# Shared expert and first routed expert in another order, with their tiles laid elsewhere, in a one-core decoder layer

## The chip, the cores and the metric

The kernel runs on one core of a Trainium2 chip. The metric is device time in microseconds (us). A core has TensorE (matrix products and transposes into eight PSUM banks), VectorE, ScalarE, GpSimd and SyncE, each with its own list of instructions in order; they wait for each other by semaphores. SyncE issues most of the transfers between HBM and SBUF; GpSimd issues those with indices (gather and scatter-add of rows).

## The reference

One decoder layer on 512 tokens of width 1024, float32: a token mixer (RG-LRU and S5), a layer norm, then a mixture of experts with a gated per-layer embedding (PLE) and a second layer norm. The change touches only the second half:

```python
y = jnp.einsum('tf,fd->td', jax.nn.silu(xt @ ws_gate) * (xt @ ws_up), ws_down)   # shared expert, F = 256
for c in range(N_EXPERTS // EXPERT_CHUNK):                                      # 64 experts, 8 per token
    ...
    hdn = jax.nn.silu(g) * u * combine[:, sl, None]
    y = y + jnp.einsum('tef,efd->td', hdn, w_down[sl])
ple = jax.nn.sigmoid(x @ ple_gate_w + ple_gate_b) * (p @ ple_w)
x = layer_norm(ALPHA * x + ffn + ple, ln2_g, ln2_b)
```

## The kernel before

SBUF is one arena of 53,200 float32 columns over 128 partitions; tiles are laid in it by hand at offsets, and many share columns at different times. The offsets that matter: `x_off` = 624, `late` = 4720, `b0` = 14960, `b1` = 26224, `m_off` = 37488, `sg_off` = 41584, `tail` = 46704. Each engine has one block of code, and its order is written out by hand.

Behind the first layer norm the tokens stand in four tiles of 128 (t = 0 to 3). TensorE then computes, per tile, the PLE gate (`ple_gate`, L923, 16 products in fp32, which the profile records as 32), the PLE value (`ple_value`, L935, 8 records), the router and the slot table (L951 to L970), and the shared expert's gate and up products (`sh_in`, L943, 16 records a tile, into banks 4, 5, 2, 3). VectorE's `ple(t)` writes `acc[:, t]`, the accumulator at `m_off`, from `ple_value(t)`; `ple_value(t)` waits for `ple(t - 1)`, as both use banks 2 and 3. The picks for the slot table are VectorE's `picks(t)`.

The shared expert goes on with silu on ScalarE (`sh_silu`, tile `sil`), its product with up on VectorE (`sh_hid`, tile `hdn`), a transpose on TensorE (`sh_turn`, through L698 like all transposes), a copy from the bank on VectorE (`sh_keep`, L1835, tile `hT`), the down product (`sh_out`, L1017, 8 records, banks 6 and 7) and two additions to `acc` on VectorE (`sh_add`). All of `sil`, `hdn` and `hT` have two buffers, at `b1` + 8192 to `b1` + 10240. SyncE then stores `acc` to `acc_dram` (L512), to which the routed experts' rows are added.

The routed experts run one after the other on up to 96 gathered rows. For expert e, with u = e mod 4: SyncE loads gate and up (2 MB, `gate_up`, L490) and down (1 MB, L493) into one of four buffers. ScalarE rounds gate and up to their high part (`gate_up_high`, four pieces of 128x1024, tile `gu_hi[u % 2]`), and VectorE subtracts to get the low part over the raw weights (`gate_up_low`). GpSimd gathers the rows, TensorE turns them (`x_turn`), and ScalarE and VectorE split them too (`rows_high`, `rows_low`). `gate_up` on TensorE is 24 products of 96 rows by 512 columns (L691 high by high, L693 high part by `rows_low`, L692 `gate_up_low` by high); then silu, the product with up and the gate, a turn (`hid_turn`), and `down` (L1057, 8 records). GpSimd adds the result rows to `acc_dram` by a scatter (`add_rows`, L642). TensorE's order in an expert is gate_up(e), x_turn(e + 1), down(e - 1), hid_turn(e). On ScalarE an expert is gate_up_high(e + 1), silu, rows_high(e + 1), y_kept(e - 1).

SyncE loads expert e + 4's gate and up when gate_up(e) is done and its down when down(e) is done, in one order. Expert 0 is loaded after the last `ple_value`, expert 1 after the last `ple`, experts 2 and 3 after the last `sh_in`.

The second high-part buffer, `gu_hi[1]`, lies at `m_off`, on the columns of `acc`. So ScalarE waits for `acc_stored` before expert(0, 0), whose first step is the high part of expert 1.

Lines of helpers: L1122 is ScalarE's `f`, L1344 and L1350 VectorE's `tt` and `stt`, L698 the transpose, L691 to L693 the three products of `mm3`.

Of the kernel before, what the change touches and what calls it, by code (L numbers as in the profile page):

```python
# [46 lines left out]
F = 256  # L47
# [25 lines left out]
def decoder_layer(nc, A, out):  # L73
# [9 lines left out]
    with ctx:  # L83
# [19 lines left out]
        def at(off, cols, rows_=P):  # L103
            assert off + cols <= COLS, (off, cols)
            return arena[0:rows_, off:off + cols]
# [8 lines left out]
        def part(name, off, n, width):  # L114

            assert off % 8 == 0 and off + n * width <= COLS
            t = nc.alloc_sbuf_tensor_at(name, (P, n * width), f32r, offset=arena_at + 4 * off)
            return t[:, :].rearrange("p (k t) -> p k t", k=n)
# [137 lines left out]
        xgT = at(tail + 4096, KD * SL).rearrange("p (k s) -> p k s", k=KD)  # L256
        xe_hi = part("rows_high", tail + 4096, KD, SL)
        xe_lo = part("rows_low", tail + 4096 + KD * SL, KD, SL)
        gu_hi = [part(f"gate_up_high{n}", o, 2 * KD, F) for n, o in enumerate((x_off, m_off))]
        gu_lo = [part(f"gate_up_low{n}", o, 2 * KD, F) for n, o in enumerate(gu_at)]  # L260
        heT = [at(b1 + 10240 + 512 * n, 2 * SL).rearrange("p (k s) -> p k s", k=2) for n in range(2)]
        hid_e = [at(tail + 5632 + n * F, F, SL) for n in range(2)]
        ohT = at(b1 + 10240, F).rearrange("p (k s) -> p k s", k=2)
        yb = [at(late + 8192 + n * D, D, SL) for n in range(2)]
        sil = [at(b1 + 8192 + n * F, F) for n in range(2)]
        hdn = [at(b1 + 8704 + n * F, F) for n in range(2)]
        hT = [at(b1 + 9216 + n * F, F).rearrange("p (k s) -> p k s", k=2) for n in range(2)]
        small = b0 + 8192

        def sc(off, cols, parts=P):  # L270
# [274 lines left out]
        def _(pool):  # L545
# [79 lines left out]
            def gather(e, u, n):  # L625

                nc.gpsimd.tensor_copy(idxcol[:, u:u + 1].bitcast(i32), idxT[:, bass.ds(e, 1)].bitcast(i32)).then_inc(S["slot_col"], 1)
                pool.wait_ge(S["slot_col"], n + 1)
                pool.sem_inc(S["col_seen"], 1)
                nc.gpsimd.indirect_dma_start(  # L630
                    out=xg[u], out_offset=None, in_=x1_dram,
                    in_offset=bass.IndirectOffsetOnAxis(ap=idxcol[:, u:u + 1].bitcast(u32), axis=0),
                    bounds_check=T - 1, oob_is_err=False).then_inc(s_gath[u], 16)
# [14 lines left out]
            pool.wait_ge(S["x1_stored"], 16 * TT)  # L648
            for u in range(4):
                gather(u, u, u)  # L650
            pool.wait_ge(S["acc_stored"], 16 * TT)

            def add_expert(i, u):
                pool.wait_ge(S["y_e_act"], 4 * i + u + 1)
# [3 lines left out]
            for u in range(4):  # L658
                pool.wait_ge(S["xT_e_put"], u + 1)
                gather(4 + u, u, 4 + u)  # L660
                if u:
                    add_expert(0, u - 1)
            with pool.Fori(1, E // 4 - 1) as i:
# [32 lines left out]
        def _(pe):  # L696
# [288 lines left out]
            ple_gate(0)  # L985
            ranks()
            ple_gate(1)
            ple_value(1)
            pe.wait_ge(S["shared_loaded"], 48)
            sh_in(0)  # L990
            ple_gate(2)
            slot_table()
            ple_value(2)
# [36 lines left out]
            def gate_up(i, u):  # L1030

                pe.wait_ge(S["gu_e_low"], 16 * i + 4 * u + 4)
                pe.wait_ge(S["xT_e_low"], 8 * i + 2 * u + 2)
                whi = gu_hi[u % 2].rearrange("p (w k) f -> p k w f", w=2)
                wlo = gu_lo[u % 4].rearrange("p (w k) f -> p k w f", w=2)
                for k in range(KD):
                    last = mm3(banks[2 + u % 2][0:SL, :], xe_hi[:, k], xe_lo[:, k], whi[:, k], wlo[:, k], k == 0, k == KD - 1)
                last.then_inc(S["g_e_put"], 1)
# [30 lines left out]
            sh_turn(1)  # L1069
            sh_out(0)  # L1070
            x_turn(0, 0)
            sh_out(1)
            sh_turn(2)
            sh_out(2)
            sh_turn(3)
            sh_out(3)
            expert(0, 0)
            pe.wait_ge(S["sh_done"], 2 * TT)
# [41 lines left out]
        def _(act):  # L1120
            def f(out_, in_, func, **kw):
                return nc.scalar.activation(out_, in_, func, **kw)  # L1122
# [152 lines left out]
            def gate_up_high(i, u):  # L1275
                act.wait_ge(s_wgu[u % 4], 32 * i + 32 * (u // 4 + 1))
                wait(act, S["g_e_put"], 4 * i + u - 1)
                for k in range(2):
                    for w in range(2):
                        ks = slice(KD * w + 4 * k, KD * w + 4 * k + 4)  # L1280
                        f(gu_hi[u % 2][:, ks], gu_raw[u % 4][:, ks], ACT.Copy).then_inc(S["gu_e_high"], 1)


            def y_kept(i, u):
# [15 lines left out]
            def sh_silu(t):  # L1300
                act.wait_ge(S["sh_put"], t + 1)
                need(act, "sh_hid", t - 1)
                f(sil[t % 2], banks[(4, 5, 2, 3)[t]][:, 0:F], ACT.Silu).then_inc(S["sh_silu"], 1)

            sh_silu(0)
            sh_silu(1)
            act.wait_ge(S["table_put"], 1)
            gate_up_high(0, 0)
            sh_silu(2)
            rows_high(0, 0)  # L1310
            sh_silu(3)
            act.wait_ge(S["acc_stored"], 16 * TT)
            for u in range(0, 5):
                expert(0, u)
            with act.Fori(1, E // 4 - 1) as i:
# [21 lines left out]
        def _(dve):  # L1337
# [5 lines left out]
            def tt(out_, a, b_, op):  # L1343
                return V_.tensor_tensor(out_, a, b_, op)  # L1344
# [506 lines left out]
            def gate_up_low(i, u):  # L1851
                for k in range(2):
                    for w in range(2):
                        ks = slice(KD * w + 4 * k, KD * w + 4 * k + 4)
                        dve.wait_ge(S["gu_e_high"], 16 * i + 4 * u + 2 * k + w + 1)
                        tt(gu_lo[u % 4][:, ks], gu_raw[u % 4][:, ks], gu_hi[u % 2][:, ks].bitcast(f32),
                           ALU.subtract).then_inc(S["gu_e_low"], 1)

            def y_kept(i, u):
# [86 lines left out]
```

## Time and profile before

| | |
|---|---|
| time, median of 3 runs | 1504.92 us (1503.16 to 1507.18) |
| profiled execution, its own time | 1510.24 us |
| its span | 1508.5 us |
| TensorE busy | 1421.3 us, 94% |
| VectorE busy | 877.7 us, 58% |
| ScalarE busy | 608.8 us, 40% |
| GpSimd busy | 431.1 us, 29% |
| mean granted TensorE clock | 0.972 |
| HBM read and written | 297.27 and 34.54 MB |

The profile is of one execution; its times are microseconds from the start of the span. "Idle before" is the time an engine stood still ahead of an instruction, and the arrow names what released it. The granted clock is a share of 2.4 GHz. A DMA share near 1 means that the 16 DMA engines are busy throughout. The span falls into the mixer (to about 613), the output projection and first norm, the PLE, router and shared expert (to about 820), the 64 experts (to about 1474) and the last norm.

### The profile page before, as it was taken

The numbers are of one execution on the slowest core, as the hardware profiler recorded it, in microseconds if no ns is written. First come the engines' busy times: TensorE is split into PE (matmuls) and PEld (weight loads), VectorE is DVE, ScalarE is ACT, GpSimd is POOL, SyncE is SP. The second block draws the span as 40 slices with busy tenths as digits, with TensorE's granted clock in tenths as the row PEclk, the third lists the DMA queues.
The fourth block names the chain that finished last, engine by engine and source line by source line (L and its number), as shares of the span: only waits on it lengthen the run. The fifth ranks groups of instructions, "written<-read, shape, count | busy, mean of one in ns | idle before, by whom it ended". The sixth has DMA issues, their size and how long they took to land.

```text
span 1508.5 us, 18646 instructions
## 1 busy us (share of the span) xinstructions
PE 1421.3 (94%) x6359; PEld 942.7 (62%) x6359; DVE 877.7 (58%) x1257; ACT 608.8 (40%) x850; POOL 431.1 (29%) x380
## 2 busy tenths in 40 slices
PE   6999899998999999999998999999999999999990
PEld 4466777675788888555544666666666666666650
DVE  3798868785600100247533667666766766666655
ACT  2215554536422222010011555555655555555440
POOL 0112525333454444000010232222233222333322
PEclk7999999999899999999999999999999999999996
DMA  8035242534233334730046799999999999999953
GB/s 246 2 112 81 74 71 72 86 63 102 63 98 98 91 98 157 306 141 12 0 169 260 256 353 354 359 367 359 363 362 363 370 367 371 359 363 367 353 160 125
DMA packets 140419, 315.77 MB, mean 209 GB/s; under 512 B 17888, under 2 KB 99472, under 8 KB 115088
## 3 DMA queue, kind: packets, MB, share of 16 engines
q1 hardware_dynamic: 126032, 281.50, 54.0%
q0 software_dynamic: 14336, 33.59, 9.5%
q8 instruction: 33, 0.54, 0.1%
q14 instruction: 18, 0.15, 0.0%
HBM read 297.27 MB, written 34.54 MB: 220 GB/s over the span
## 4 chain that ended last, share of the span: by engine, by line
PE 74%; issue 8%; DVE 7%; DMA 3%; POOL 2%; DVEq 2%; ACT 1%; POOLq 1%; SPq 0%; ACTq 0%
PE bank L691 14%; PE bank L693 14%; PE bank L692 14%; PE bank L1057 14%; PE bank L698 5%; PE bank L909 4%; DVE arena L1344 3%; DVEq L1341 2%; PE bank L923 2%; PE bank L943 2%; DMA gate_up<-moe_w_up_in 2%; POOL wa_low L563 1%; PE bank L935 1%; PE bank L1017 1%; PE bank L824 1%
## 5 line engine op out<-in xcount | busy, mean ns | idle before, releaser
L1344 DVE TENSOR_TENSOR gate_up_low<-gate_up,gate_up_high 128x1024 fp32r<-128x1024 f32 x256 | 296.5, 1219 | 105.3 <-ACT gate_up_high L1122 105.3
L1122 ACT ACTIVATE gate_up_high<-gate_up 128x1024 fp32r<-128x1024 f32 x256 | 249.6, 1047 | 78.4 <-DMA gate_up<-moe_w_up_in 57.9
L1122 ACT ACTIVATE arena<-bank 96x512 f32<-96x512 f32 (+5 forms) x248 | 131.4, 553 | 363.9 <-PE bank L1057 137.0
L1057 PE MATMUL bank<-down,arena 128*96 128x512 f32 x512 | 230.4, 592 | 1.0 <-DVE arena L1876 1.0
L1344 DVE TENSOR_TENSOR arena<-arena 128x512 f32<-128x512 f32 (+12 forms) x296 | 211.9, 747 | 19.5 <-ACT arena L1122 5.0
L691 PE MATMUL bank<-gate_up_high,rows_high 128*96 128x512 f32 x512 | 206.7, 404 | 1.2 <-DVE rows_low L1344 1.0
L693 PE MATMUL bank<-gate_up_high,rows_low 128*96 128x512 f32 x512 | 203.1, 397 | 0.0
L692 PE MATMUL bank<-gate_up_low,rows_high 128*96 128x512 f32 x512 | 201.6, 394 | 0.0
L698 PEld LDWEIGHTS bank<-arena 96*128 96x128 f32 (+5 forms) x1001 | 129.5, 189 | 58.6 <-issue 45.8
L563 POOL TENSOR_TENSOR wb_low<-arena,wb_high 128x1024 fp32r<-128x1024 f32 (+1 forms) x40 | 105.6, 2639 | 151.9 <-ACT wb_high L1122 151.8
L1057 PEld LDWEIGHTS bank<-down,arena 128*96 128x96 f32 x512 | 80.3, 167 | 103.5 <-issue 103.4
L698 PE MATMUL bank<-arena 96*128 96x96 f32 (+5 forms) x1001 | 129.1, 269 | 11.2 <-DMA arena<-x_in 4.7
L639 POOL COPY arena<-arena 96x1 int32 (+1 forms) x64 | 17.4, 272 | 346.2 <-DMA acc_dram<-arena 326.9
L1350 DVE SCALAR_TENSOR_TENSOR arena<-bank,arena 128x511 f32<-128x511 f32 (+3 forms) x44 | 32.2, 747 | 139.5 <-PE bank L693 137.2
L563 POOL TENSOR_TENSOR wa_low<-arena,wa_high 128x1024 fp32r<-128x1024 f32 x24 | 60.7, 2542 | 181.3 <-ACT wa_high L1122 181.3
L642 POOL DMA_INDIRECT acc_dram<-arena x64 | 94.6, 1478 | 58.2 <-POOL arena L639 53.1
L1122 ACT ACTIVATE arena<-arena 128x512 f32<-128x512 f32 (+5 forms) x54 | 31.6, 610 | 186.1 <-DVE arena L1344 87.7
L691 PEld LDWEIGHTS bank<-gate_up_high,rows_high 128*96 128x96 f32 x512 | 84.9, 166 | 33.8 <-issue 2.3
L693 PEld LDWEIGHTS bank<-gate_up_high,rows_low 128*96 128x96 f32 x512 | 83.0, 162 | 36.5
L1122 ACT ACTIVATE wb_high<-arena 128x1024 fp32r<-128x1024 f32 (+1 forms) x40 | 45.8, 1144 | 148.5 <-DMA arena<-w_glu_in 80.2
L692 PEld LDWEIGHTS bank<-gate_up_low,rows_high 128*96 128x96 f32 x512 | 83.4, 163 | 32.5 <-issue 0.7
L1862 DVE COPY arena<-bank 96x512 f32<-96x512 f32 x64 | 44.0, 687 | 91.6 <-PE bank L1057 74.3
(149 smaller groups left out, 2159.9 us busy)
## 6 DMA issues: line engine op xcount, KB each, us to landing
gate_up<-moe_w_gate_in SPq DMA_DIRECT2D x64, 1024.0 KB
gate_up<-moe_w_up_in SPq DMA_DIRECT2D x64, 1024.0 KB
down<-moe_w_down_in SPq DMA_DIRECT2D x64, 1024.0 KB
arena<-w_in_in SPq DMA_DIRECT2D x40, 512.0 KB, 4.1
arena<-w_glu_in SPq DMA_DIRECT2D x16, 512.0 KB, 4.0
arena<-w_lru_out_in SPq DMA_DIRECT2D x8, 768.0 KB, 4.8
arena<-x_in SPq DMA_DIRECT2D x8, 512.0 KB, 5.1
arena<-w_in_in SPq DMA_DIRECT2D x2, 2048.0 KB, 12.3
```

The costliest lines, as they stand in the source:

```text
L563: nc.gpsimd.tensor_tensor(lo, w, hi.bitcast(f32), ALU.subtract).then_inc(S["w_split"], 1)
L642: nc.gpsimd.indirect_dma_start(out=acc_dram, out_offset=bass.IndirectOffsetOnAxis(ap=idxcol[:, 4:5].bitcast(u32), axis=0), in_=yb[buf], in ...
L691: mm(dst, w_hi, v_hi, start=start, stop=False)
L692: mm(dst, w_hi, v_lo, start=False, stop=False)
L693: return mm(dst, w_lo, v_hi, start=False, stop=stop)
L698: return nc.tensor.transpose(dst, src, ident[0:n, 0:n])
L909: last = mm(banks[n % 4][:, :], merged[:, k, t * P:(t + 1) * P], wout[:, k, hf * 512:(hf + 1) * 512], start=(k == 0), stop=(k == KD - 1))
L1057: last = mm(banks[5 + hf][0:SL, :], heT[u % 2][:, k], dn[u % 4][:, k, hs], start=(k == 0), stop=(k == 1))
L1122: return nc.scalar.activation(out_, in_, func, **kw)
L1344: return V_.tensor_tensor(out_, a, b_, op)
L1350: return V_.scalar_tensor_tensor(out_, a, s, b_, op0, op1)
L1862: V_.tensor_copy(yb[u % 2][:, 512:1024], banks[6][0:SL, :]).then_inc(S["y_e_dve"], 1)
```

## The change

The order of some steps is changed on TensorE, ScalarE and GpSimd, and some tiles are laid elsewhere.

- TensorE: `sh_in(0)` stands ahead of `ple_value(1)`; `sh_turn(2)` ahead of `sh_out(1)` and `sh_turn(3)` ahead of `sh_out(2)`.
- ScalarE: `sh_silu(3)` stands ahead of `rows_high(0, 0)`; the wait for `acc_stored` is gone; a wait for all four `ple_val` stands ahead of `sh_silu(0)`.
- GpSimd: the wait for `acc_stored` stands behind the gathers of experts 4 and 5, ahead of the first scatter-add, instead of ahead of both gathers.
- Layout: `gu_hi[1]` lies in two parts of 2048 columns, its gate half at `b1` + 8192 and its up half at `sg_off` (7168 columns apart; the halves of `gu_hi[0]` are 2048 apart). These columns held the PLE's tokens and turned tokens and the shared tiles, and the first norm's two parameters and a pick tile. `sil`, `hdn` and `hT` lie at `late` + 8192 to `late` + 10240, on the columns of the PLE weights (`plew`) and, later, of `yb`.

```diff
--- before.py
+++ after.py
@@ -256,15 +256,16 @@
         xgT = at(tail + 4096, KD * SL).rearrange("p (k s) -> p k s", k=KD)
         xe_hi = part("rows_high", tail + 4096, KD, SL)
         xe_lo = part("rows_low", tail + 4096 + KD * SL, KD, SL)
-        gu_hi = [part(f"gate_up_high{n}", o, 2 * KD, F) for n, o in enumerate((x_off, m_off))]
+        gu_hi = [part(f"gate_up_high{n}", o, 2, w)[:, :, 0:KD * F].rearrange("p w (k f) -> p w k f", k=KD)
+                 for n, (o, w) in enumerate(((x_off, KD * F), (b1 + 8192, sg_off - b1 - 8192)))]
         gu_lo = [part(f"gate_up_low{n}", o, 2 * KD, F) for n, o in enumerate(gu_at)]
         heT = [at(b1 + 10240 + 512 * n, 2 * SL).rearrange("p (k s) -> p k s", k=2) for n in range(2)]
         hid_e = [at(tail + 5632 + n * F, F, SL) for n in range(2)]
         ohT = at(b1 + 10240, F).rearrange("p (k s) -> p k s", k=2)
         yb = [at(late + 8192 + n * D, D, SL) for n in range(2)]
-        sil = [at(b1 + 8192 + n * F, F) for n in range(2)]
-        hdn = [at(b1 + 8704 + n * F, F) for n in range(2)]
-        hT = [at(b1 + 9216 + n * F, F).rearrange("p (k s) -> p k s", k=2) for n in range(2)]
+        sil = [at(late + 8192 + n * F, F) for n in range(2)]
+        hdn = [at(late + 8704 + n * F, F) for n in range(2)]
+        hT = [at(late + 9216 + n * F, F).rearrange("p (k s) -> p k s", k=2) for n in range(2)]
         small = b0 + 8192
 
         def sc(off, cols, parts=P):
@@ -648,7 +649,6 @@
             pool.wait_ge(S["x1_stored"], 16 * TT)
             for u in range(4):
                 gather(u, u, u)
-            pool.wait_ge(S["acc_stored"], 16 * TT)
 
             def add_expert(i, u):
                 pool.wait_ge(S["y_e_act"], 4 * i + u + 1)
@@ -658,6 +658,8 @@
             for u in range(4):
                 pool.wait_ge(S["xT_e_put"], u + 1)
                 gather(4 + u, u, 4 + u)
+                if u == 1:
+                    pool.wait_ge(S["acc_stored"], 16 * TT)
                 if u:
                     add_expert(0, u - 1)
             with pool.Fori(1, E // 4 - 1) as i:
@@ -985,9 +987,9 @@
             ple_gate(0)
             ranks()
             ple_gate(1)
-            ple_value(1)
             pe.wait_ge(S["shared_loaded"], 48)
             sh_in(0)
+            ple_value(1)
             ple_gate(2)
             slot_table()
             ple_value(2)
@@ -1031,7 +1033,7 @@
 
                 pe.wait_ge(S["gu_e_low"], 16 * i + 4 * u + 4)
                 pe.wait_ge(S["xT_e_low"], 8 * i + 2 * u + 2)
-                whi = gu_hi[u % 2].rearrange("p (w k) f -> p k w f", w=2)
+                whi = gu_hi[u % 2].rearrange("p w k f -> p k w f")
                 wlo = gu_lo[u % 4].rearrange("p (w k) f -> p k w f", w=2)
                 for k in range(KD):
                     last = mm3(banks[2 + u % 2][0:SL, :], xe_hi[:, k], xe_lo[:, k], whi[:, k], wlo[:, k], k == 0, k == KD - 1)
@@ -1069,10 +1071,10 @@
             sh_turn(1)
             sh_out(0)
             x_turn(0, 0)
+            sh_turn(2)
             sh_out(1)
-            sh_turn(2)
+            sh_turn(3)
             sh_out(2)
-            sh_turn(3)
             sh_out(3)
             expert(0, 0)
             pe.wait_ge(S["sh_done"], 2 * TT)
@@ -1278,7 +1280,7 @@
                 for k in range(2):
                     for w in range(2):
                         ks = slice(KD * w + 4 * k, KD * w + 4 * k + 4)
-                        f(gu_hi[u % 2][:, ks], gu_raw[u % 4][:, ks], ACT.Copy).then_inc(S["gu_e_high"], 1)
+                        f(gu_hi[u % 2][:, w, 4 * k:4 * k + 4], gu_raw[u % 4][:, ks], ACT.Copy).then_inc(S["gu_e_high"], 1)
 
 
             def y_kept(i, u):
@@ -1302,14 +1304,14 @@
                 need(act, "sh_hid", t - 1)
                 f(sil[t % 2], banks[(4, 5, 2, 3)[t]][:, 0:F], ACT.Silu).then_inc(S["sh_silu"], 1)
 
+            act.wait_ge(S["ple_val"], TT)
             sh_silu(0)
             sh_silu(1)
             act.wait_ge(S["table_put"], 1)
             gate_up_high(0, 0)
             sh_silu(2)
+            sh_silu(3)
             rows_high(0, 0)
-            sh_silu(3)
-            act.wait_ge(S["acc_stored"], 16 * TT)
             for u in range(0, 5):
                 expert(0, u)
             with act.Fori(1, E // 4 - 1) as i:
@@ -1853,7 +1855,7 @@
                     for w in range(2):
                         ks = slice(KD * w + 4 * k, KD * w + 4 * k + 4)
                         dve.wait_ge(S["gu_e_high"], 16 * i + 4 * u + 2 * k + w + 1)
-                        tt(gu_lo[u % 4][:, ks], gu_raw[u % 4][:, ks], gu_hi[u % 2][:, ks].bitcast(f32),
+                        tt(gu_lo[u % 4][:, ks], gu_raw[u % 4][:, ks], gu_hi[u % 2][:, w, 4 * k:4 * k + 4].bitcast(f32),
                            ALU.subtract).then_inc(S["gu_e_low"], 1)
 
             def y_kept(i, u):
```

## Rows read from the trace of the kernel before

**Rows 1.** Stretches: span, busy time (count) by engine, clock, DMA share, GB/s.

```profile
780.00:790.00 10.00, 10.00 (x24) 4.37 (x23) 4.86 (x7) 4.28 (x5) 0.00 (x0) 1.00 1.01 428
830.00:840.00 10.00, 8.48 (x28) 5.71 (x29) 6.77 (x9) 3.61 (x4) 0.37 (x1) 0.66 0.48 186
840.00:850.00 10.00, 10.00 (x44) 6.24 (x43) 6.49 (x9) 5.64 (x8) 3.33 (x3) 1.00 0.46 173
1220.00:1230.00 10.00, 10.00 (x43) 6.31 (x42) 6.90 (x9) 5.17 (x9) 2.83 (x4) 1.00 1.02 361
```

**Rows 2.** TensorE in order of time: start, duration, operation, [idle before, releaser].

```profile
718.83 6.35 PE L935 MATMUL bank<-arena 128*128 128x512 f32 x8 [4.74 <-DVE arena L1350]
...
756.29 3.70 PE L935 MATMUL bank<-arena 128*128 128x512 f32 x8
...
777.19 20.76 PE L943 MATMUL bank<-gate_up,arena 128*128 128x512 f32 x48
...
798.71 3.70 PE L1017 MATMUL bank<-down,arena 128*128 128x512 f32 x8 [0.28 <-DVE arena L1835]
...
805.64 5.37 PE L1017 MATMUL bank<-down,arena 128*128 128x512 f32 x8 [2.38 <-DVE arena L1344]
...
812.44 3.67 PE L1017 MATMUL bank<-down,arena 128*128 128x512 f32 x8 [1.20 <-DVE arena L1344]
...
820.65 0.80 PE L691 MATMUL bank<-gate_up_high,rows_high 128*96 128x512 f32 x1
...
826.61 1.02 PE L698 MATMUL bank<-arena 96*128 96x96 f32 x8
...
832.11 0.71 PE L691 MATMUL bank<-gate_up_high,rows_high 128*96 128x512 f32 x1 [0.43 <-DVE rows_low L1344]
...
840.75 3.60 PE L1057 MATMUL bank<-down,arena 128*96 128x512 f32 x8
...
850.82 3.60 PE L1057 MATMUL bank<-down,arena 128*96 128x512 f32 x8
```

**Rows 3.** ScalarE in order of time, high parts of the weights in the loop.

```profile
1036.99 3.90 ACT L1122 ACTIVATE gate_up_high<-gate_up 128x1024 fp32r<-128x1024 f32 x4 [0.69 <-DMA gate_up<-moe_w_up_in]
...
1432.75 3.90 ACT L1122 ACTIVATE gate_up_high<-gate_up 128x1024 fp32r<-128x1024 f32 x4 [1.46 <-DMA gate_up<-moe_w_up_in]
```

**Rows 4.** SyncE in order of time, loads of experts 4 and 5.

```profile
826.96 0.36 SPq L490 DMA_DIRECT2D gate_up<-moe_w_gate_in  x1
...
844.38 0.33 SPq L493 DMA_DIRECT2D down<-moe_w_down_in  x1
```

**Rows 5.** Stretches behind two gaps of TensorE, columns as in Rows 1.

```profile
718.80:722.00 3.20, 3.17 (x4) 1.51 (x5) 3.05 (x4) 0.00 (x0) 0.00 (x0) 0.50 0.00 0
805.60:808.00 2.40, 2.36 (x4) 1.10 (x5) 1.43 (x3) 0.00 (x0) 0.00 (x0) 0.61 1.01 427
```

**Rows 6.** VectorE in order of time: last pick, third shared copy, low part of rows.

```profile
735.71 0.96 DVE L1344 TENSOR_TENSOR arena<-arena 128x768 f32<-128x768 f32 x1
...
811.28 0.42 DVE L1835 COPY arena<-bank 128x256 f32<-128x256 f32 x1 [4.25 <-PE bank L698]
...
830.96 1.01 DVE L1344 TENSOR_TENSOR rows_low<-bank,rows_high 128x384 fp32r<-128x384 f32 x2
```

**Rows 7.** ScalarE in order of time around the start of the loop.

```profile
784.86 3.90 ACT L1122 ACTIVATE gate_up_high<-gate_up 128x1024 fp32r<-128x1024 f32 x4 [0.21 <-DMA gate_up<-moe_w_up_in]
...
804.05 0.39 ACT L1122 ACTIVATE arena<-bank 128x256 f32<-128x256 f32 x1
824.91 3.90 ACT L1122 ACTIVATE gate_up_high<-gate_up 128x1024 fp32r<-128x1024 f32 x4 [20.46 <-DMA acc_dram<-arena]
...
840.95 0.87 ACT L1122 ACTIVATE rows_high<-bank 128x384 fp32r<-128x384 f32 x2 [0.48 <-PE bank L698]
```

**Rows 8.** Groups of the page: two kinds of product in the loop.

```profile
L691 PE MATMUL bank<-gate_up_high,rows_high 128*96 128x512 f32 x512 | 206.7, 404 | 1.2 <-DVE rows_low L1344 1.0
...
L692 PE MATMUL bank<-gate_up_low,rows_high 128*96 128x512 f32 x512 | 201.6, 394 | 0.0
```

## The prediction

> **What bounds the kernel now.** I read the stretches of ten microseconds first, then TensorE's order of work around the change, then the other engines beside it. The reader should see three things. First, in the routed loop TensorE is busy for all of every stretch and so are the DMA engines: 10.00 of 10.00 us with a DMA share of 1.02 at 361 GB/s [rows 1]. One expert costs 10.07 us of TensorE (850.82 less 840.75, the starts of two successive down products) [rows 2]. Second, the weight stream is slightly slower than that. The high parts begin to wait for their weights at 1036.99, by 0.69 us, and near the end they wait 1.46 us [rows 3]; the high part of 1432.75 is the one on the chain that ended last. So the loop is a tie of TensorE and DMA, and the DMA wins it narrowly in the last few experts. Neither is touched by the change. Third, ahead of the loop neither is full: the DMA share is 0.48 and 0.46 between 830 and 850 [rows 1], and TensorE has gaps of 4.74, 2.38 and twice 1.20 us (the second of these, before sh_out(3), is not shown) and one of over 4 us before 832.11 [rows 2]. That is the stretch the change rewrites.
>
> Does time won ahead of the loop survive to the end? It does if the stream moves with it. SyncE issues expert 4's gate and up at 826.96, when expert 0's products are done, and its down weights and expert 5's gate and up from 844.38, when down(0) is done [rows 4] (down runs 840.75 + 3.60 = 844.35 [rows 2]). Only from there is the queue always full. Both issues hang on TensorE's progress, so the stream and the loop move together.
>
> **The change, part by part.** Sums are of this execution: span 1508.5, its own time 1510.24; the median of the three runs is 1504.92, 5.3 lower. I take the difference off the median, since the removed gaps are order of work and not noise.
>
> A. sh_in(0) before ple_value(1). ple_value(1) starts at 718.83 after 4.74 us of waiting for ple(0) on VectorE, and takes 6.35 against 3.70 for the same eight records at 756.29 [rows 2], because the granted clock is 0.50 (1.2 GHz) after that gap [rows 5]. sh_in(0) has 16 records; 48 of them take 20.76 [rows 2], so it is 6.92 us and covers the 4.74 wholly: TensorE reaches ple_value(1) at 714.09 + 6.92 = 721.0, after 718.8. Gone: 4.74 + 2.65 = 7.39; by the starts of the products around it a little more. I take 7.5. What is late next? slot_table would be reached about 721.0 + 3.46 + 13.84 = 738.3 (eight records, then 32 of ple_gate(2), at 20.76/48 each), and the last pick ends 735.71 + 0.96 = 736.7 [rows 6], 1.6 us earlier: no new wait. ple(1) and the gate biases on VectorE come earlier than their new use too. Everything to the end of sh_in(3), the gathers and the first expert loads moves 7.5 earlier.
>
> B. sh_turn(t+1) before sh_out(t), and silu(3) before the rows' high part. From sh_out(0) at 798.71 to the first record of gate_up(0) at 820.65 are 21.94 us [rows 2]. Waits of 2.38, 1.20 and 1.20 stand in it, and sh_out(1) ran at clock 0.61 for 5.37 instead of 3.67 [rows 2, 5]. Each 1.20 is the round trip turn, copy by VectorE (the one at 811.28 [rows 6]), out; with the turn one product ahead the copy lies under a product. The 2.38 is VectorE waiting for silu(3), which ScalarE ran at 804.05, after the rows' high part that needs x_turn [rows 7]. sh_in(3) is done at 797.9 (777.19 + 20.76), so silu(3) now runs about 798.3 and the copies follow at once. VectorE's order does not change: rows_low(0) stands before the third copy. In this trace's clock x_turn would end about 803.1, rows_high 804.2, rows_low 804.9, the third copy 805.3; sh_out(2) wants it at about 807. The adds to the accumulator (under 0.7 each) end before the bank's next product: 809.6 against 810.5 for the tightest. Left: 4 x 3.46 (eight records at 20.76/48) + x_turn 0.9 + two turns 0.4 = 15.1. Gone: 21.94 - 15.1 = 6.8.
>
> C. The second high-part buffer. ScalarE's high part of expert 1 starts at 824.91 after 20.46 us of waiting for the accumulator's store [rows 7], because the buffer lay on the accumulator. Expert 0's high part starts at 784.86, with its weights just in [rows 7]; expert 1's are next in the queue, two more loads after expert 0's down, some 3.1 MB or 8 us later. So the high part of expert 1 finds them and can run right after rows_high(0), about 804.3 to 808.2. VectorE's low part takes under 5 us (it cannot start before the first quarter of the high part of 824.91 is done, 825.9, and rows_low at 830.96 stands behind it [rows 6]); it follows the last add, about 814.3 to 819.2, beside gate_up(0). gate_up(0) would start at 813.8 and end at 819.4; 5.61 is its length at full clock (10.07 - 3.60 - 0.86). What is late next is the rows of expert 1: x_turn 0.9, rows_high starting right behind it, rows_low half a microsecond after rows_high starts (the first half of its 0.87 [rows 7]), 1.15 from rows_low's start to gate_up(1) (830.96 to 832.11) [rows 2, 6]: 2.7 us together, of which 1.35 (behind the turn of the hidden rows) is idle at one go. From gate_up(0) to gate_up(1): 5.61 + 2.7 = 8.3 instead of 11.46. Gone: 3.1.
>
> D. Clock behind that gap. gate_up(1) took 7.78 (832.11 to 840.75, less x_turn 0.86), while the clock of 830:840 was 0.66 on the mean, that is 1.2 GHz for two thirds of it [rows 1, 2]. A gap of 1.20 us was followed by a product of 3.67, so at full clock; one of 2.38 by 5.37 [rows 2]. 1.35 is nearer to 1.20, so I take full clock: 7.78 - 5.61 = 2.2 gone. If not, 0.
>
> Priced at nothing. ScalarE's new wait for ple_val before sh_silu(0): ple_value(3) is over before sh_in(1) starts, and sh_silu(1), the high part of expert 0 and VectorE's sh_hid queue behind it with over 5 us to spare (bounds: 0, and 0 as long as the delay is under those 5 us). GpSimd's wait for the accumulator's store, behind gather 5 instead of before gather 4: the last add ends near 814.3 in this trace's clock and the store some 3 us later, add_expert(0) wants it after 832; what is queued behind it is that addition and gather 6, neither sooner needed. The split buffer: ScalarE writes and VectorE reads runs of 1024 elements as before, and a matmul reads two runs of 256 as before, only further apart; no row shows such a distance, so bounds are 0 and, taking the spread between kinds of product in the loop (404 and 394 ns [rows 8]), 10 ns on 16 records of 32 experts = 5 us. I take 0, since the two pieces are already apart today.
>
> Sum: 7.5 + 6.8 + 3.1 + 2.2 = 19.6. 1504.9 - 19.6 = 1485.3. Its own range, 1482 to 1488.5: half a microsecond on each term, and a few parts in a thousand on a stream of 590 us.
>
> **Rivals.**
> 1. The stream is the bound and does not move by all of it. Between the first expert load and 844.38 the queue has to carry fourteen loads of 1.05 MB (three for each of experts 0 to 3, two for expert 4) = 14.7 MB, 2.1 MB of accumulator and six gathers of at most 0.39 MB: 19.2 MB. The first is issued when ple_value(3) is done, at 777.2 [rows 2], so it had 67.2 us and has 67.2 - 12.1 = 55.1 us in the new order (B, C and D; A moves both ends). At the 428 GB/s of 780:790 [rows 1] that is 45 us: it fits with 10 to spare, but its middle is bunched (five loads at once after sh_in(3)). For it: the loop's DMA share is over 1 [rows 1]. Against: the idle between 830 and 850 [rows 1]. Up to 5 us back: 1490. Chance 0.12. The Trainium skill, "DMA: Bandwidth & Descriptors", Specifications, gives about 358 GB/s as the limit of HBM for one core. By that the loop's 361 is the ceiling, which the trace bears out, but the front's 428 lies above it. An estimate by that page: 19.2 MB take 53.6 of the 55.1 us, so the front would be just full and 1 or 2 us come back, about 1487.
> 2. The 1.35 us gap lowers the clock as the 2.38 one did: D is nothing, 1485.3 + 2.2 = 1487.5. Chance 0.12.
> 3. The reorder does not do what it says: VectorE's unchanged order (rows_low before the third copy, an add before the fourth) makes sh_out(2) or sh_out(3) wait, which leaves two gaps of 1.2 to 2.4 us and one lowered clock, 4 us: 1489. Against it is the 1.7 us margin above. Chance 0.06.
> 4. Slower. The far-apart halves of gate_up_high1 make each product that reads them dearer. It has 16 records in 32 experts = 512; the 19.6 won are used up at 38 ns each, a tenth of the 404 ns [rows 8], and at 60 ns (31 us) it is 1516. For it: TensorE has no slack in the loop [rows 1]. Against: the same two-run read exists already. Chance 0.03.
>
> **How the numbers follow.** Forecast 0.67, rivals 0.12, 0.12, 0.06, 0.03. A time 0.3% from 1504.9 (4.5 us) is about what a measurement can tell: faster is below 1500.4. All cases but the fourth lie there: faster 0.95, same 0.02 (rival 4 at about its break-even), slower 0.03. The range goes from 1480.5 (forecast with rows a little better in each term) to 1491, over rivals 1 to 3.
>
> **What the profile of after would show.** A: ple_value(1) without a gap, 3.4 to 3.7 us, sh_in(3) ending near 790.4. B: sh_out(0) to gate_up(0) in about 15 us, no gap over 0.5. C: expert 1's high part starting near 797 with no wait for acc_dram; gate_up(1) about 8.3 us after gate_up(0), near 814.5. D: clock 1.00 there. The loop then at 10.07 per expert and down(0) ending near 824.7 (844.35 less 19.6). Wrong if the high parts wait for weights well before twenty experts are done, if the last experts come slower than 10.4 each, or if records of L691 and L693 differ between odd and even experts.

## The result, and the profile after

The changed kernel takes 1484.99 us (median of 6 runs, 1482.43 to 1488.57) against 1505.09 for the kernel before (6 runs, 1503.16 to 1507.18): 0.9868 of its time, 95% interval 0.9854 to 0.9881, or 20.1 us less. The forecast was 1485.3 and 19.6 us less.

From the page of the changed kernel: span, TensorE's busy time, its granted clock and the DMA share in forty slices, and the chain that ended last.

```profile
span 1482.8 us, 18646 instructions
...
PE   6999899999899999999999999999999999999990
...
PEclk8999999999899999999999999999999999999995
DMA  9035242525133333750038899999999999999943
...
PE 81%; DVE 7%; issue 4%; DVEq 3%; POOL 2%; DMA 2%; POOLq 1%; ACT 1%; SPq 0%
```

The chain is 81% TensorE and holds no wait for weights, where the chain of before had 23.34 us of one. Line numbers are two higher than before: L693 to L695 are the three products and L700 the turn; L925, L937, L945, L1019 and L1059 are the gate, the value, the shared gate and up, the shared down and the expert's down product; L1124 is ScalarE's helper, L1346 and L1837 are VectorE's.

TensorE in order of time, to be read against [rows 2]:

```profile
696.70 13.95 PE L925 MATMUL bank<-arena 128*128 128x512 f32 x32
710.49 7.03 PE L945 MATMUL bank<-gate_up,arena 128*128 128x512 f32 x16
717.36 3.60 PE L937 MATMUL bank<-arena 128*128 128x512 f32 x8
...
766.10 20.76 PE L945 MATMUL bank<-gate_up,arena 128*128 128x512 f32 x48
...
787.61 3.70 PE L1019 MATMUL bank<-down,arena 128*128 128x512 f32 x8 [0.28 <-DVE arena L1837]
791.15 1.28 PE L700 MATMUL bank<-arena 96*128 96x96 f32 x10
792.27 3.60 PE L1019 MATMUL bank<-down,arena 128*128 128x512 f32 x8
...
795.93 7.03 PE L1019 MATMUL bank<-down,arena 128*128 128x512 f32 x16
802.40 0.79 PE L693 MATMUL bank<-gate_up_high,rows_high 128*96 128x512 f32 x1
...
808.37 1.62 PE L700 MATMUL bank<-arena 96*128 96x96 f32 x10
811.11 0.45 PE L693 MATMUL bank<-gate_up_high,rows_high 128*96 128x512 f32 x1 [1.13 <-DVE rows_low L1346]
...
817.58 3.60 PE L1059 MATMUL bank<-down,arena 128*96 128x512 f32 x8
...
827.64 3.60 PE L1059 MATMUL bank<-down,arena 128*96 128x512 f32 x8
```

In this stretch TensorE has no gap left but 0.28 us and the one of 1.13 ahead of the second expert's first product (811.11). `ple_value(1)` (717.36) takes 3.60 instead of 6.35. The shared down products stand back to back, the last two merged in one row (795.93, 7.03 us).

ScalarE, against [rows 7]. The silu of tile 3 runs at 786.90, ahead of the rows' high part, and expert 1's high part at 792.96, without a wait:

```profile
786.90 0.38 ACT L1124 ACTIVATE arena<-bank 128x256 f32<-128x256 f32 x1 [6.48 <-PE bank L945]
792.21 0.87 ACT L1124 ACTIVATE rows_high<-bank 128x384 fp32r<-128x384 f32 x2 [4.92 <-PE bank L700]
792.96 3.90 ACT L1124 ACTIVATE gate_up_high<-gate_up 128x1024 fp32r<-128x1024 f32 x4
...
809.42 0.87 ACT L1124 ACTIVATE rows_high<-bank 128x384 fp32r<-128x384 f32 x2 [0.48 <-PE bank L700]
```

VectorE, against [rows 6]: the last pick, the third and fourth shared copies, and the low parts of expert 1's weights and rows.

```profile
732.28 0.96 DVE L1346 TENSOR_TENSOR arena<-arena 128x768 f32<-128x768 f32 x1
...
793.67 0.41 DVE L1837 COPY arena<-bank 128x256 f32<-128x256 f32 x1
...
796.51 0.42 DVE L1837 COPY arena<-bank 128x256 f32<-128x256 f32 x1
...
803.61 4.62 DVE L1346 TENSOR_TENSOR gate_up_low<-gate_up,gate_up_high 128x1024 fp32r<-128x1024 f32 x4
...
809.95 1.02 DVE L1346 TENSOR_TENSOR rows_low<-bank,rows_high 128x384 fp32r<-128x384 f32 x2 [0.49 <-ACT rows_high L1124]
```

SyncE, against [rows 4]: expert 4's gate and up, and its down weights once down(0) is done.

```profile
808.71 0.36 SPq L491 DMA_DIRECT2D gate_up<-moe_w_gate_in  x1
...
821.21 0.33 SPq L494 DMA_DIRECT2D down<-moe_w_down_in  x1
```

The stretches can be compared between the starts of six steps, in each execution from its own start of `ple_gate(1)` (700.13 before, 696.70 after). "The last down" is the down product of expert 63.

| stretch of TensorE | before | after | less | forecast |
|---|---|---|---|---|
| ple_gate(1) to sh_out(0) | 98.58 | 90.91 | 7.67 | A 7.5 |
| sh_out(0) to gate_up(0) | 21.94 | 14.79 | 7.15 | B 6.8 |
| gate_up(0) to gate_up(1) | 11.46 | 8.71 | 2.75 | C 3.1 |
| gate_up(1) to down(0) | 8.64 | 6.47 | 2.17 | D 2.2 |
| together | 140.62 | 120.88 | 19.74 | 19.6 |
| down(0) to the last down | 630.03 | 627.62 | 2.41 | 0 |
| start to ple_gate(1) | 700.13 | 696.70 | 3.43 | 0 |

The two spans differ by 25.7 us, more than the 20.1 of the medians. The last two rows are why. Neither belongs to the change: in the experiments the start to ple_gate(1) differs by up to 4.1 us and the loop by up to 1.7 us between two profiles of one kernel.

### The profile page after: what moved, and what is told of

Same layout as the page of the kernel before. It is cut to its first block, busy times and chain, and to the rows that moved or that the text cites. A ratio compares the mean times of both kernels' runs of the same rounds, so it can differ in the third digit from the quotient of the medians.

```text
span 1482.8 us, 18646 instructions
## 1 busy us (share of the span) xinstructions
PE 1408.8 (95%) x6359; PEld 935.6 (63%) x6359; DVE 885.1 (60%) x1257; ACT 610.5 (41%) x850; POOL 458.1 (31%) x380
## 4 chain that ended last, share of the span: by engine, by line
PE 81%; DVE 7%; issue 4%; DVEq 3%; POOL 2%; DMA 2%; POOLq 1%; ACT 1%; SPq 0%
PE bank L693 15%; PE bank L1059 15%; PE bank L695 15%; PE bank L694 14%; PE bank L700 6%; DVE arena L1346 4%; PE bank L925 4%; PE bank L911 4%; PE bank L727 3%; DVEq L1343 3%; PE bank L945 2%; POOLq L599 1%; POOL arena L600 1%; PE bank L937 1%; PE bank L1019 1%
## 5 line engine op out<-in xcount | busy, mean ns | idle before, releaser
L1346 DVE TENSOR_TENSOR gate_up_low<-gate_up,gate_up_high 128x1024 fp32r<-128x1024 f32 x256 | 296.4, 1220 | 39.3 <-ACT gate_up_high L1124 39.3
L1124 ACT ACTIVATE arena<-bank 96x512 f32<-96x512 f32 (+5 forms) x248 | 131.8, 555 | 417.5 <-PE bank L1059 169.8
L1124 ACT ACTIVATE gate_up_high<-gate_up 128x1024 fp32r<-128x1024 f32 x256 | 249.3, 1047 | 0.1
L1059 PE MATMUL bank<-down,arena 128*96 128x512 f32 x512 | 230.4, 592 | 1.0 <-DVE arena L1878 1.0
L1346 DVE TENSOR_TENSOR arena<-arena 128x512 f32<-128x512 f32 (+12 forms) x296 | 213.9, 754 | 19.4 <-ACT arena L1124 4.8
L693 PE MATMUL bank<-gate_up_high,rows_high 128*96 128x512 f32 x512 | 206.0, 402 | 1.1 <-DVE rows_low L1346 1.1
L695 PE MATMUL bank<-gate_up_high,rows_low 128*96 128x512 f32 x512 | 202.5, 395 | 0.0
L700 PEld LDWEIGHTS bank<-arena 96*128 96x128 f32 (+5 forms) x1001 | 126.7, 186 | 55.9 <-issue 47.3
L1059 PEld LDWEIGHTS bank<-down,arena 128*96 128x96 f32 x512 | 80.3, 167 | 103.5 <-issue 103.4
L640 POOL COPY arena<-arena 96x1 int32 (+1 forms) x64 | 47.4, 740 | 311.6 <-DMA acc_dram<-arena 282.8
L700 PE MATMUL bank<-arena 96*128 96x96 f32 (+5 forms) x1001 | 126.7, 265 | 8.5 <-DMA arena<-x_in 5.1
L643 POOL DMA_INDIRECT acc_dram<-arena x64 | 99.6, 1556 | 58.2 <-POOL arena L640 54.9
L1124 ACT ACTIVATE wb_high<-arena 128x1024 fp32r<-128x1024 f32 (+1 forms) x40 | 45.8, 1144 | 148.4 <-DMA arena<-w_glu_in 79.9
L695 PEld LDWEIGHTS bank<-gate_up_high,rows_low 128*96 128x96 f32 x512 | 82.2, 161 | 36.5
L693 PEld LDWEIGHTS bank<-gate_up_high,rows_high 128*96 128x96 f32 x512 | 84.4, 165 | 32.9 <-issue 1.5
L1124 ACT ACTIVATE arena<-arena 128x512 f32<-128x512 f32 (+5 forms) x54 | 31.6, 610 | 178.6 <-DVE arena L1652 86.6
```

The source lines that it names most:

```text
L640: nc.gpsimd.tensor_copy(idxcol[:, 4:5].bitcast(i32), idxT[:, bass.ds(e, 1)].bitcast(i32)).then_inc(S["sc_col"], 1)
L643: nc.gpsimd.indirect_dma_start(out=acc_dram, out_offset=bass.IndirectOffsetOnAxis(ap=idxcol[:, 4:5].bitcast(u32), axis=0), in_=yb[buf], in ...
L693: mm(dst, w_hi, v_hi, start=start, stop=False)
L695: return mm(dst, w_lo, v_hi, start=False, stop=stop)
L700: return nc.tensor.transpose(dst, src, ident[0:n, 0:n])
L1059: last = mm(banks[5 + hf][0:SL, :], heT[u % 2][:, k], dn[u % 4][:, k, hs], start=(k == 0), stop=(k == 1))
```

## The experiments

In the experiments all stretches are read as in the table above. "Before" beside a group of runs is the kernel before, run again with them on the same chip.

**Each part alone.** The whole change is A, B and C together. `a_only`:

```diff
             ple_gate(1)
-            ple_value(1)
             pe.wait_ge(S["shared_loaded"], 48)
             sh_in(0)
+            ple_value(1)
             ple_gate(2)
```

> The kernel before with part A alone: sh_in(0) ahead of ple_value(1). My theory (the gap of 4.74 us goes whole, and with it the lowered clock behind it): ple_value(1) without a gap and in 3.6 to 3.7 us, 7.5 us off the time, 1497.6. Rival 1 (the weight stream sets the end and moves by less): the same local picture, but less than 4 us off the time, with longer waits for weights in the last experts.

`b_only`:

```diff
             x_turn(0, 0)
+            sh_turn(2)
             sh_out(1)
-            sh_turn(2)
+            sh_turn(3)
             sh_out(2)
-            sh_turn(3)
             sh_out(3)
...
             sh_silu(2)
+            sh_silu(3)
             rows_high(0, 0)
-            sh_silu(3)
             act.wait_ge(S["acc_stored"], 16 * TT)
```

> The kernel before with part B alone: each shared turn one product ahead, silu(3) ahead of the high part of expert 0's rows. Theory: sh_out(0) to gate_up(0) in 15.1 us instead of 21.9, the accumulator stored 6.8 us earlier and with it expert 1's high part, 6.8 off the time, 1498.3. Rival 3 (VectorE's unchanged order makes the later products wait): 17.5 to 19 us between the two, 3 to 4.5 off.

`c_only` is the changed kernel with those two edits undone. Against the kernel before (the new place of the shared tiles, the reads of the split buffer and GpSimd's later wait are left out here):

```diff
-        gu_hi = [part(f"gate_up_high{n}", o, 2 * KD, F) for n, o in enumerate((x_off, m_off))]
+        gu_hi = [part(f"gate_up_high{n}", o, 2, w)[:, :, 0:KD * F].rearrange("p w (k f) -> p w k f", k=KD)
+                 for n, (o, w) in enumerate(((x_off, KD * F), (b1 + 8192, sg_off - b1 - 8192)))]
...
+            act.wait_ge(S["ple_val"], TT)
             sh_silu(0)
...
             sh_silu(3)
-            act.wait_ge(S["acc_stored"], 16 * TT)
```

> The kernel before with part C alone: second high-part buffer and shared tiles laid elsewhere, no wait for the accumulator's store on ScalarE, that of GpSimd two gathers later. Theory: gate_up(1) starts 8.3 us after gate_up(0) instead of 11.5 (3.1) and at full clock (2.2), 5.3 off the time, 1499.8. If the gap of 1.35 us still lowers the clock: 3.1 off, 1502. If the far-apart halves cost TensorE anything (rival 4): records of L691 and L693 longer in odd experts than in even ones, and a time above 1505.

`ab` has the first two diffs on the kernel before.

> Both reorders, the layout and its waits as before (C undone). Theory: parts add up, 7.5 + 6.8 = 14.3 off, 1490.8, and expert 1's high part still waits for the accumulator's store. If the parts share a cover (one gap hidden by either): less than 12 off.

The four ran on one chip, with before at 1505.64:

| kernel | median, us | of before, 95% | ple_gate(1) to sh_out(0) | to gate_up(0) | to gate_up(1) | to down(0) | together | less than before |
|---|---|---|---|---|---|---|---|---|
| a_only | 1496.16 | 0.9940 (0.9918 to 0.9962) | 90.91 | 21.95 | 11.43 | 9.02 | 133.31 | 7.31 |
| b_only | 1499.12 | 0.9960 (0.9946 to 0.9973) | 98.52 | 14.79 | 13.21 | 7.95 | 134.47 | 6.15 |
| c_only | 1503.02 | 0.9982 (0.9969 to 0.9995) | 98.51 | 21.94 | 8.73 | 8.03 | 137.21 | 3.41 |
| ab | 1494.07 | 0.9926 (0.9900 to 0.9951) | 90.91 | 14.79 | 13.08 | 8.41 | 127.19 | 13.43 |

The stretches repeat to 0.1 us where the code ahead of them is the same, while whole times of one kernel lie up to 9 us apart (`a_only`, 1492.18 to 1501.39). So the parts are read from the stretches; the medians (9.5, 6.5, 2.6 and 11.6 less) have intervals that hold them. A is as forecast in its own stretch. B wins the whole 7.15 in its own stretch, so rival 3 is out, but gives back 1.75 between gate_up(0) and gate_up(1) while the buffer still lies on the accumulator. ScalarE and SyncE of `b_only`:

```profile
813.67 3.90 ACT L1122 ACTIVATE gate_up_high<-gate_up 128x1024 fp32r<-128x1024 f32 x4 [15.33 <-DMA acc_dram<-arena]
```

```profile
797.33 11.97 SPq L512 DMA_DIRECT2D acc_dram<-arena  x4
809.35 0.43 SPq L493 DMA_DIRECT2D down<-moe_w_down_in  x1
```

The last store of the accumulator is issued at about 809.3 and the high part starts at 813.67, 4.4 us later; before it was 2.6 us (822.3 to 824.91 [rows 7]). The stores now come sooner behind the five loads of experts 2 and 3 that SyncE issues ahead of them. The two microseconds ahead of the last store, before and then in `b_only` (columns as in [rows 1]):

```profile
820.00:822.00 2.00, 2.00 (x8) 1.01 (x7) 0.91 (x2) 0.00 (x0) 0.00 (x0) 1.00 0.05 18
```

```profile
808.00:810.00 2.00, 2.00 (x10) 1.38 (x9) 0.69 (x1) 0.00 (x0) 0.00 (x0) 1.00 1.04 426
```

The DMA engines were nearly idle (0.05) in the one and full (1.04) in the other. That the store queues behind the loads fits this, but no run took it apart. C alone gives 3.41 instead of 5.3: its own 2.73 is there, but gate_up(1) still runs slowly, 8.03 to down(0) instead of 6.47. The three parts alone make 16.9, together 19.7. Of the 2.9 between, 1.0 is what B alone lost (1.75 to the store, less 0.7 by which its gate_up(1) to down(0) was shorter), and C takes the store off this path; 1.6 is C's slow gate_up(1), and 0.4 A's (9.02 instead of 8.64). `ab` has 13.4 of the 14.3 forecast for the same reason. The slow product is the next question.

**Why the clock stays up.** The changed kernel and `c_only` have the same gap ahead of gate_up(1). TensorE of `c_only`:

```profile
803.38 5.37 PE L1019 MATMUL bank<-down,arena 128*128 128x512 f32 x8 [2.38 <-DVE arena L1346]
...
827.11 0.45 PE L693 MATMUL bank<-gate_up_high,rows_high 128*96 128x512 f32 x1 [1.13 <-DVE rows_low L1346]
...
835.14 3.60 PE L1059 MATMUL bank<-down,arena 128*96 128x512 f32 x8
```

Its stretches behind that gap (span, busy time of each engine, granted clock, DMA share, GB/s), and then those of the changed kernel:

```profile
829.00:831.00 2.00, 2.00 (x7) 1.25 (x6) 2.00 (x3) 1.07 (x2) 0.00 (x0) 0.50 1.00 422
833.00:835.00 2.00, 2.00 (x14) 1.60 (x13) 0.11 (x1) 0.38 (x1) 0.00 (x0) 1.00 0.00 0
```

```profile
811.10:813.00 1.90, 1.89 (x8) 1.36 (x9) 1.86 (x3) 1.90 (x3) 0.38 (x1) 1.00 1.03 427
813.00:815.00 2.00, 2.00 (x10) 1.43 (x9) 2.00 (x3) 1.08 (x2) 0.00 (x0) 1.00 1.00 422
```

Behind 1.13 us of waiting the clock is 0.50 (1.2 GHz) in one and 1.00 (2.4 GHz) in the other. Is that chance? Both were profiled again, unedited, as `c_only2` and `after2`.

> Part C alone once more. Its first profile had the same gap of 1.13 us ahead of gate_up(1) as the changed kernel, but the clock at half behind it (gate_up(1) to down(0) 8.03 us against 6.47). If the two gaps of 1.20 us that B removes are what makes the difference: half again. If chance: full in one of the two.

> The changed kernel once more, for a second profile. If it is the change that frees the loop from waits for weights (none over 0.1 us in its first profile): none again. If chance: 20 to 60 us of them as in the four kernels between. The clock behind the gap of 1.13 us ahead of gate_up(1): 1.00 again if what went before it decides, 0.5 in some executions if chance.

gate_up(1) to down(0) took 8.04 and 6.47, within 0.01 of the first profiles, so it is not chance of an execution but something in the kernel. Two kernels part the gaps: `c_turns` (C with only the turns of B) and `c_silu` (C with only its silu order).

`c_turns`, against `c_only`:

```diff
             x_turn(0, 0)
+            sh_turn(2)
             sh_out(1)
-            sh_turn(2)
+            sh_turn(3)
             sh_out(2)
-            sh_turn(3)
```

> Part C with B's turns but not its silu order: the two gaps of 1.20 us ahead of gate_up(0) go where a turn can run early, the one of 2.38 stays. If the gaps of 1.20 are what leaves the clock at half behind the 1.13 gap: gate_up(1) to down(0) in 6.47 us as in the changed kernel. If the 2.38 one is: 8.0 as in C alone.

`c_silu`, against `c_only`:

```diff
             sh_silu(2)
+            sh_silu(3)
             rows_high(0, 0)
-            sh_silu(3)
```

> Part C with B's silu order but not its turns: the gap of 2.38 us goes or falls to 1.2, three gaps near 1.20 stay in front of gate_up(0). If the gaps of 1.20 leave the clock low later: 8.0 from gate_up(1) to down(0). If only the 2.38 one did: 6.47. The clock behind the first gap should stay full, so sh_out(0) to gate_up(0) falls from 21.9 to about 19.

TensorE of `c_turns`, then of `c_silu`:

```profile
803.81 5.37 PE L1019 MATMUL bank<-down,arena 128*128 128x512 f32 x8 [2.12 <-DVE arena L1346]
...
832.46 3.60 PE L1059 MATMUL bank<-down,arena 128*96 128x512 f32 x8
```

```profile
796.68 3.63 PE L1019 MATMUL bank<-down,arena 128*128 128x512 f32 x8
...
801.74 3.67 PE L1019 MATMUL bank<-down,arena 128*128 128x512 f32 x8 [1.21 <-DVE arena L1346]
...
806.84 3.67 PE L1019 MATMUL bank<-down,arena 128*128 128x512 f32 x8 [1.20 <-DVE arena L1346]
...
825.12 3.60 PE L1059 MATMUL bank<-down,arena 128*96 128x512 f32 x8
```

With the turns alone the long gap stays (2.12 us, the product behind it 5.37 us), and gate_up(1) to down(0) takes 8.03. With the silu order alone the long gap is gone, two of 1.20 stay, no product is slow, and it takes 6.46. sh_out(0) to gate_up(0) is 18.84 and 17.66, against 14.79 without gaps. So the two gaps of 1.20 cost 2.87 together, 0.2 us each above their length, and no clock. The gap of 2.12 costs 4.05: its length, 1.7 us at half clock right behind it, and 0.2. It also goes with a second fall of the clock behind the 1.13 us gap, 21 to 24 us later, which costs another 1.6. D's gain is therefore not C's alone: it needs B's silu order. A is not needed for it: A's gap of 4.76 us stands in `c_silu` as in `c_only` and `c_turns`. The rule for the second fall stays open. Shown is only that behind the 1.13 us gap the clock fell in three executions with the long gap ahead (`c_only` twice, `c_turns`) and in none of four without it (the changed kernel twice, `c_silu`, and `after_thin` below with 6.49).

**Does the weight stream bound the loop?** The prediction said that it wins narrowly in the last experts. `before2` is the kernel before again.

> The kernel before once more, for a second profile. If the loop's late stalls and ScalarE's waits for weights (57.9 us in 41 waits in the first profile) are the kernel's: 40 to 60 us of waits again, the last experts over 10.07 us apart. If they are chance of one execution: clearly other figures.

ScalarE's waits for weights, as total, count and longest, in `before2` and `after2`:

```profile
ACT gate_up_high L1122 <- DMA gate_up<-moe_w_up_in: 58.0, 32, 2.8
```

```profile
ACT gate_up_high L1124 <- DMA gate_up<-moe_w_up_in: 67.1, 41, 2.8
```

Before had 57.9 us of them and after none in their first profiles; `c_only` had 29.9 and then 0.3, and `c_silu` has 85.1. So they are chance of an execution and not the change's. Where they come they begin some twenty experts in (1035.47 in `after2`, 1036.99 in the first profile of before). Nearly all are absorbed ahead of TensorE: down(0) to the last down took 630.03 and 629.05 in the two profiles of before, 627.62 and 629.32 in those of after. Two kernels cut the stream; they leave most of the down weights unloaded and so don't compute the layer:

```diff
             def load_down(e, u, done):
-                sp.dma_start(dn_row[u], w_down_e[bass.ds(e, 1)].rearrange("o p x -> p (o x)")).then_inc(done, 16)
+                cut = slice(0, 2 * D) if isinstance(e, int) else slice(0, 128)
+                sp.dma_start(dn_row[u][:, cut], w_down_e[bass.ds(e, 1)].rearrange("o p x -> p (o x)")[:, cut]).then_inc(done, 16)
```

> The changed kernel with the down weights of experts 4 to 63 loaded only in their first 128 of 2048 columns (these experts' down products then use left-over weights, so their part of the result is not computed; all instructions and waits stay): the stream carries 31% less. Theory (TensorE bounds the loop, the stream costs 0 to 2 us in its last experts): loop of 627.6 us from down(0) to the last down, no waits for weights, 1484 within 2. Rival 1 (the stream bounds): more than 4 us faster than the changed kernel.

> The kernel before with the same cut of the down loads of experts 4 to 63 (their part of the result is not computed). Theory: the loop falls from 629 to 630 us to 627.6, 1.4 to 2.4 us, 1503.5; the front is as before, since its wait is for the accumulator's store behind additions and not for weights. Rival 1: more than 4 us faster.

A hundred microseconds of the loop, `after_thin` and then the changed kernel:

```profile
1000.00:1100.00 100.00, 100.00 (x417) 62.35 (x416) 70.23 (x90) 56.05 (x79) 42.16 (x40) 1.00 0.80 266
```

```profile
1000.00:1100.00 100.00, 100.00 (x420) 62.74 (x419) 70.21 (x90) 56.09 (x80) 35.40 (x40) 1.00 1.02 366
```

The stream falls from 366 to 266 GB/s and its share from 1.02 to 0.80. The loop takes 627.62 us in both thin kernels, the very figure of the changed kernel's first profile. Medians are 1486.43 for `after_thin` (0.9878, 0.9859 to 0.9897), not faster than the changed kernel's 1484.99 and just outside the 1484 within 2 that was expected, and 1505.79 for `before_thin` (0.9999, 0.9987 to 1.0010), beside 1505.46 for before: the 1.4 to 2.4 us expected of `before_thin` are in its loop (627.62 for 629 to 630) and can't be seen in its median, whose runs go from 1501.6 to 1507.05. TensorE bounds the loop; the stream adds 0 to 2.4 us to an execution (627.62 to 630.03). Rival 1 is out, for before as for after.

The kernels profiled in one execution each took 1505.03 (`before2`), 1488.11 (`after2`), 1500.91 (`c_only2`), 1499.59 (`c_turns`) and 1494.60 us (`c_silu`); with one time each, their stretches alone are compared.

**The last gap.** `fill` puts work of the shared expert into the gaps that are left.

```diff
             sh_turn(1)
+            x_turn(0, 0)
             sh_out(0)
-            x_turn(0, 0)
...
             sh_out(2)
-            sh_out(3)
-            expert(0, 0)
+            gate_up(0, 0)
+            x_turn(0, 1)
+            sh_out(3)
+            hid_turn(0, 0)
+            gate_up(0, 1)
+            x_turn(0, 2)
             pe.wait_ge(S["sh_done"], 2 * TT)
-            for u in range(1, 5):
+            down(0, 0)
+            hid_turn(0, 1)
+            for u in range(2, 5):
                 expert(0, u)
...
             sh_add(2)
-            sh_add(3)
-            for u in range(0, 5):
+            gate_up_low(0, 1)
+            dve.wait_ge(S["silu_e"], 1)
+            stt(hid_e[0], hid_e[0], gateT[:, 0:1], banks[2][0:SL, F:2 * F], ALU.mult, ALU.mult).then_inc(S["hid_e"], 1)
+            rows_low(0, 1)
+            sh_add(3)
+            dve.wait_ge(S["hT_e_put"], 1)
+            V_.tensor_copy(heT[0], banks[4][:, 0:2 * SL].rearrange("p (k x) -> p k x", k=2)).then_inc(S["hT_e_kept"], 1)
+            for u in range(1, 5):
                 expert(0, u)
```

> The changed kernel with its last TensorE gaps filled: x_turn(0) ahead of sh_out(0), and sh_out(3) behind gate_up(0) and x_turn(1), with VectorE's low part of expert 1 ahead of its last shared additions. Theory: the gaps of 0.28 and 1.35 us plus 0.3 go, sh_out(0) to down(0) 1.9 us shorter than in the changed kernel, no gap that could lower the clock, 1483.1. If the stream bound the end: no change from 1485.

TensorE of `fill`, from sh_out(0) to down(0):

```profile
791.15 3.63 PE L1019 MATMUL bank<-down,arena 128*128 128x512 f32 x8
...
801.53 0.79 PE L693 MATMUL bank<-gate_up_high,rows_high 128*96 128x512 f32 x1
...
807.50 1.02 PE L700 MATMUL bank<-arena 96*128 96x96 f32 x8
808.36 3.62 PE L1019 MATMUL bank<-down,arena 128*128 128x512 f32 x8
...
811.96 0.45 PE L693 MATMUL bank<-gate_up_high,rows_high 128*96 128x512 f32 x1
...
818.45 3.60 PE L1059 MATMUL bank<-down,arena 128*96 128x512 f32 x8
```

There is no gap left here; the product at 811.96 follows at once. `ple_gate(1)` to down(0) takes 118.63 us, 2.25 less than in the changed kernel, where 1.9 were expected. The median is 1483.65 (0.9850, 0.9828 to 0.9872, beside before at 1506.2). That interval overlaps the changed kernel's, so the step is shown by the stretch, and by the time only as not contradicted.

## Why the prediction was right

**What bounds the kernel.** Half right. TensorE does bound the loop, at 10.06 us an expert. That "the DMA wins it narrowly in the last few experts" is wrong as a property of the kernel: it was one execution's, and with a quarter less traffic the loop is as long as it is without waits. A DMA share of 1.02 and waits of an engine ahead of TensorE were read as a bound, though TensorE itself had one listed wait, of 0.5 us, between 850 and 1445 of that profile. What hid the waits is argued and not tested: expert 3's low part ends at 827.4 in the changed kernel and its first product starts at 831.2, 3.8 us later, and no wait of a high part was longer than 3.0 us. No number of the sum hung on it, since loop and stream moved together, as forecast: down(0) ends at 821.2 and SyncE issues expert 4's down weights at 821.21.

**A.** 7.67 for 7.5. The slot table did not wait: it follows the gate product at once (734.52), and the last pick ends at 733.24, 1.3 us earlier where the prediction had 1.6.

**B.** 7.15 for 6.8. The copies came at 793.67 and 796.51, both under a product. Four products were put at 3.46 each, start to start; the two merged ones take 6.47 (795.93 to 802.40), not 6.92, since the first record of gate_up(0) starts 0.4 us early and is 0.79 long where one inside is 0.40.

**C.** 2.75 for 3.1. The chain behind x_turn was right: x_turn (808.37), rows_high 1.05 later, rows_low 0.53 after that, gate_up(1) 1.16 after that, 2.74 together. The prediction has 2.7, though its terms as written (0.9, 0.5 and 1.15) make 2.55. What is off is gate_up(0), 5.97 (802.40 to 808.37) instead of 5.61. The rows of before had it: 826.61 less 820.65 is 5.96 [rows 2]. The 5.61 is a product inside the loop. So B's surplus and C's shortfall are one 0.4 us, booked on the wrong side of gate_up(0)'s start, and they cancel: B and C together are 9.90 for 9.9.

**D.** 2.17 for 2.2. The gap came out at 1.13 us for 1.35, and the guess that it leaves the clock alone held, so rival 2 is out. The reason given, that 1.35 is nearer to 1.20 than to 2.38, was incomplete: the same gap is followed by half clock in `c_only`. The prediction booked D as following from C; it follows from C and B's silu order together, and that both stood in one change was luck as far as this reasoning goes. The rows of before were also read too shortly here: the "one of over 4 us before 832.11" is two gaps, 0.43 and, ahead of the turn of the hidden rows, 3.46. So before, the half clock of gate_up(1) followed 3.46 us of idle:

```profile
831.09 0.59 PE L698 MATMUL bank<-arena 96*128 96x96 f32 x2 [3.46 <-DVE arena L1350]
```

**Priced at nothing.** ScalarE's new wait ended at 766.3, with 6.5 us of idle before its next step. GpSimd's wait delayed nothing: the first scatter's column is copied at 822.17, after down(0). The far-apart halves cost nothing: down products follow each other every 10.06 us through even and odd experts alike, and the loop is no longer than with the halves adjacent (627.6 in before's own thin run). Rival 4 is out.

**The stream ahead of the loop.** By the 358 GB/s of the Trainium skill ("DMA: Bandwidth & Descriptors", Specifications) one or two microseconds were to come back. None did (19.74 against 19.6), and the changed kernel again moved 428 GB/s there:

```profile
770.00:780.00 10.00, 10.00 (x25) 4.50 (x24) 5.05 (x5) 4.29 (x5) 0.00 (x0) 1.00 1.01 428
```

So in this one-core kernel the figure is no ceiling for such a stretch.

## What to carry to other kernels

Price a reorder by the gaps it closes, start to start, and add what the clock lost behind each; then ask of the transfers only whether their issue hangs on the same engine, because then they move along. A saturated queue and waits of a helper engine do not make a bound while the engine behind has no gaps: cut the traffic and look. Here a gap of 2.12 us was worth almost twice its length (4.05), and closing it also kept the clock up behind a later gap that looked unrelated (1.6).

## What the runs showed of the hardware

- The same gap of TensorE (1.13 us, behind two turns) was followed by full clock in four executions and by half clock in three; what differed was a gap of 2.12 to 2.38 us that had ended 21 to 24 us earlier.
- Profiles of one kernel differ by several microseconds where it is not edited: `ple_gate(1)` starts at 693.7 to 700.1 in the fourteen profiles, while the stretch from there to sh_out(0) repeats to 0.1 us (90.9 or 98.5 to 98.6, and 91.3 in `fill`, where sh_out(0) stands later). So two microseconds of a change are seen in such a stretch and hardly in the median of a few runs.
